# Splits, norms and first gates interleaved between the last expert and the convolution of a two-block transformer kernel

## The reference, cut to what matters

```python
h = h + hier_moe(rmsnorm(h, ffn_norm_g), ...)    # 32 experts, 2 per token
x = rmsnorm(h, final_norm_g)                     # "first norm" of the join
h = rms_norm(x, mix_norm)                        # "second norm" of the join
a, g = jnp.split(h @ w_in + b_in, 2, axis=-1)
u = a * jax.nn.sigmoid(g)
y = silu(layer_norm(causal_conv_31_taps(u) + conv_b)) @ w_out + b_out
x = x + y
x = x + square(relu(rms_norm(x, mlp_norm) @ w1)) @ w2
```

## Time and profile before

| what | value |
| --- | --- |
| median of three runs | 2309.69 us (2308.45 to 2314.13) |
| the profiled execution | 2312.9 us, span 2311.1 us |
| TensorE, busy | 2106.1 us, 91% |
| VectorE, busy | 1263.3 us, 55% |
| ScalarE, busy | 976.7 us, 42% |
| mean granted TensorE clock | 0.959 |
| bytes moved by DMA | 352.96 MB, mean 153 GB/s |

### The profile page before, as it was taken

The page is one execution under the profiler, slowest core; times in us unless marked ns, Lnnn a source line. Parts: engine busy times, 40 slices in busy tenths (PEclk is TensorE's granted clock), DMA queues, the critical chain, the costliest instruction groups (busy, mean ns, idle before and its releaser), DMA issues.

```text
span 2311.1 us, 28597 instructions
## 1 busy us (share of the span) xinstructions
PE 2106.1 (91%) x11035; PEld 1088.9 (47%) x11035; DVE 1263.3 (55%) x1346; ACT 976.7 (42%) x1252; POOL 258.5 (11%) x263
## 2 busy tenths in 40 slices
PE   7988989898499999999936999959899999999999
PEld 5444446644244444444413565634444444444444
DVE  5234247644799898899965253384443343333432
ACT  5212227622388888888754252362322111211210
POOL 0000130000133323233200000041000000000000
PEclk9999999999699999999967999979999999999999
DMA  6110310051399999999974152234211011020001
GB/s 259 37 37 37 91 28 1 19 203 74 120 408 400 402 390 386 385 387 385 371 302 149 50 193 81 76 98 156 73 40 70 36 73 36 36 73 36 36 0 73
DMA packets 74717, 352.96 MB, mean 153 GB/s; under 512 B 16336, under 2 KB 23120, under 8 KB 42064
## 3 DMA queue, kind: packets, MB, share of 16 engines
q1 hardware_dynamic: 56304, 305.21, 34.4%
q0 software_dynamic: 18336, 46.69, 6.2%
HBM read 326.67 MB, written 29.36 MB: 154 GB/s over the span
## 4 chain that ended last, share of the span: by engine, by line
PE 75%; DVE 9%; DMA 7%; issue 4%; ACT 2%; SPq 2%; ACTq 0%; POOL 0%; DVEq 0%; POOLq 0%
PE ps L408 20%; PE ps L410 20%; PE ps L409 20%; DMA stage<-in_w_up 6%; PE pt L408 2%; PE pt L409 2%; PE pt L410 2%; DVE split L538 2%; PE pt L462 1%; DVE cols L1457 1%; SPq L629 1%; PE pt L1870 1%; PE pt L2029 1%; PE pt L2031 1%; PE pt L2030 1%
## 5 line engine op out<-in xcount | busy, mean ns | idle before, releaser
L408 PE MATMUL ps<-xt,split 128*128 128x512 f16 (+1 forms) x992 | 373.6, 377 | 18.0 <-issue 10.4
L408 PE MATMUL ps<-split,xt 128*128 128x512 f16 x928 | 354.5, 382 | 25.5 <-DMA xt<-arena 19.5
L409 PE MATMUL ps<-xt,split 128*128 128x512 f16 (+1 forms) x992 | 373.5, 377 | 0.0
L410 PE MATMUL ps<-xt,split 128*128 128x512 f16 (+1 forms) x992 | 373.3, 376 | 0.0
L409 PE MATMUL ps<-split,xt 128*128 128x512 f16 x928 | 354.5, 382 | 0.0
L410 PE MATMUL ps<-split,xt 128*128 128x512 f16 x928 | 354.3, 382 | 0.0
L538 DVE SCALAR_TENSOR_TENSOR split<-stage,split 128x2048 f16<-128x2048 f32 x128 | 289.6, 2284 | 5.4 <-ACT split L534 5.2
L534 ACT ACTIVATE split<-stage 128x2048 f16<-128x2048 f32 x128 | 243.8, 1909 | 80.5 <-DMA stage<-in_w_up 35.7
L408 PE MATMUL ps<-split,arena 128*128 128x512 f16 x512 | 194.0, 379 | 0.0
L409 PE MATMUL ps<-split,arena 128*128 128x512 f16 x512 | 194.0, 379 | 0.0
L410 PE MATMUL ps<-split,arena 128*128 128x512 f16 x512 | 194.0, 379 | 0.0
(11 more groups left out here) (292 smaller groups left out, 3150.4 us busy)
## 6 DMA issues: line engine op xcount, KB each, us to landing
stage<-in_w_gate SPq DMA_DIRECT2D x64, 1024.0 KB, 11.1
stage<-in_w_up SPq DMA_DIRECT2D x64, 1024.0 KB, 12.1
arena<-in_w_down SPq DMA_DIRECT2D x64, 1024.0 KB, 11.9
stage<-in_w_mlp SPq DMA_DIRECT2D x32, 1024.0 KB, 5.5
arena<-in_conv_taps POOLq DMA_DIRECT2D x32, 576.0 KB, 4.4
stage<-in_w_dense_a SPq DMA_DIRECT2D x16, 1024.0 KB, 7.7
stage<-in_w_dense_b SPq DMA_DIRECT2D x12, 1024.0 KB, 9.9
resid<-in_x SPq DMA_DIRECT2D x16, 512.0 KB, 4.4
```

Of the source, the lines that this page charges most:

```text
L408: nc.tensor.matmul(out_ap, lh, rh, start=start, stop=False)
L409: nc.tensor.matmul(out_ap, lh, rl, start=False, stop=False)
L410: return nc.tensor.matmul(out_ap, ll, rh, start=False, stop=stop)
```

## The change

Four things in the join, and what they need. (1) The units 2 and 3 are loaded ahead of 0 and 1 and split inside the last expert: their high halves before `hTh`, the other two high halves behind it, the four low halves behind the hidden rows' low half. (2) Groups 64 to 67 are cut into pieces of 256 tokens (`piece`), so that products begin when tiles 0 and 1 are there. (3) The lists `JOIN_ACT`, `JOIN_DVE` and `JOIN_PE` write the order out by hand: gates 0 to 3, which read the banks, stand between and behind the norms, and taps 0 to 2 behind gate 2 and gate 3. (4) `UN[k]` is tile k of `H`, so steps k = 0 to 3 need only the stores of tiles 0 to 3 (the store semaphore is now two) and steps k >= 4 no longer wait for `xn`. The squares of the statistics, which were written to `junk` (now in use by the gates), go to slot 3 of `stage`; unit 7 is therefore loaded after the last statistic. SyncE mixes y loads with the stores, and loads the tables before them. A Sqrt on one element stands ahead of the statistics.

```diff
-        UN = [f16_rows(H[:, 4 + k, :]) for k in range(4)] + [f16_rows(xn[:, k % 2, :]) for k in range(4, KT)]
+        UN = [f16_rows(H[:, k, :]) for k in range(KT)]
...
+        JOIN_ACT = seq("one:0 one:1 two:0 two:1 hi:0 hi:1 one:2 two:2 one:3 hi:2 two:3 hi:3 one:4 two:4 one:5 hi:4 "
+                       "two:5 gate:0 one:6 hi:5 two:6 gate:1 one:7 hi:6 two:7 hi:7 gate:2 taps:0 taps:1 gate:3 taps:2")
+        JOIN_DVE = seq("add:0 add:1 one:0 one:1 two:0 two:1 add:2 lo:0 lo:1 one:2 add:3 two:2 one:3 lo:2 two:3 add:4 "
+                       "lo:3 one:4 add:5 two:4 one:5 add:6 lo:4 two:5 gate:0 one:6 add:7 lo:5 two:6 gate:1 one:7 lo:6 "
+                       "two:7 lo:7 gate:2 taps:0 taps:1 gate:3 taps:2")
...
@@ SyncE
-            for m in range(SLOTS):
+            for m in (2, 3, 0, 1):
                 load_b(sp, m)
+            sp.dma_start(tables, a["conv_tables"]).then_inc(s_tab, 16)
+            sp.dma_start(blk, a["c_blk"]).then_inc(s_tab, 16)
...
+            sp.wait_ge(s_moe, 1)
+            for t in range(6):
+                load_y(t)
+            store_x2(0)
+            store_x2(1)
+            load_y(6)
+            store_x2(2)
+            load_y(7)
+            for t in range(3, TT):
+                store_x2(t)
             for m in range(SLOTS, 8):
+                if m == 7:
+                    sp.wait_ge(s_std, 4 * TT + 1)
                 load_b(sp, m)
@@ ScalarE, in the body of an expert
+                else:
+                    for m in (2, 3):
+                        hi_b(act, m)
                 act.wait_ge(s_ht, e + 1)
...
                 nc.scalar.activation(hTh, PS[:, 3, :].rearrange("p (k t) -> p k t", k=4), ACT.Copy)\
                     .then_inc(s_hh, 1)
+                if last and q:
+                    act.wait_ge(s_u, NE)
+                    for m in (0, 1):
+                        hi_b(act, m)
@@ ScalarE, after the experts
-            for m in range(SLOTS):
...
-                hi_b(act, m)
...
+            squares = wstage(3)[:, 0:D]
+            act.wait_ge(s_wo[3], RB + 1)
+            ch.done(nc.scalar.activation(std[:, 0:1], eps, ACT.Sqrt))
...
@@ in input_hi
-                if k >= 4:
-                    act.wait_ge(s_tr, 4 * TT)
-                if k >= 6:
-                    act.wait_ge(s_rb[k - 2], 16 * PH * PH)
+                act.wait_ge(s_x2s[k // 4], 16 * 4)
+                act.wait_ge(s_xn, 3 * TT + k + 1)
@@ VectorE, in the body of an expert
+                if last and q:
+                    for m in (2, 3, 0, 1):
+                        lo_b(dve, m)
@@ TensorE
-            for t in range(TT // 2):
-                transposes(pe, 3, t, from_xn)
+            def piece(g, q):
+                pe.wait_ge(s_free[g % 4], g // 4)
+                pe.wait_ge(s_xl, 3 * TT + 2 * q + 2)
+                c0, tk = (g - 64) // 2 * P, slice(256 * q, 256 * q + 256)
+                for ui in range(2):
+                    u = 2 * (g % 2) + ui
+                    pe.wait_ge(s_wo[u], RB + 1)
+                    for kk in range(UK):
+                        k, c = ui * UK + kk, slice(kk * UC + c0, kk * UC + c0 + P)
+                        i = product(pe, PS[:, g % 4, tk], whi(u)[:, c], wlo(u)[:, c], XH[:, k, tk], XL[:, k, tk],
+                                    k == 0, k == KT - 1)
+                if q:
+                    i.then_inc(s_full[g % 4], 1)
+
+            JOIN_PE = seq("tr:0 tr:1 64:0 65:0 tr:2 66:0 67:0 tr:3 64:1 tr:4 65:1 66:1 tr:5 67:1")
...
             for p, (k, th) in enumerate(GATED):
+                if p < 2:
+                    continue
                 pe.wait_ge(s_xl, 3 * TT + (TT if th else TT // 2))
                 for i in range(2):
                     u = 4 * (k // 4) + 2 * i
                     group_b(pe, 64 + 2 * p + i, (u, u + 1), True, k % 4, th)
-                    for t in {0: (4,), 1: (5, 6), 2: (7,)}.get(2 * p + i, ()):
-                        transposes(pe, 3, t, from_xn)
+                    if p in (2, 3) and i == 0:
+                        transposes(pe, 3, 4 + p, from_xn)
```

More of the change, by code:

```diff
@@ L934, in _ @@
                 phased(k)
[L935 removed]
+            for i in range(2):
+                sp.wait_ge(s_x2s[i], 16 * 4)
             x2_phase = x2_rows.rearrange("(h p r) d -> r h p d", h=2, r=PH)
@@ L1302, in conv_read @@
                         hi_b(act, SPLIT_WITH[k] + q)
-            for n in range(3):
-                taps_hi(n)
-            for p in range(len(GATED)):
+            for what, t in JOIN_ACT:
+                if what == "one":
+                    act.wait_ge(s_cmb, 2 * t + 2)
+                    norm_stats(act, ch, t, squares)
+                elif what == "two":
+                    act.wait_ge(s_x2, t + 1)
+                    norm_stats(act, ch, t, squares)
+                elif what == "hi":
+                    xt_hi(act, 3, t)
+                elif what == "taps":
+                    taps_hi(t)
+                else:
+                    gate(t)
+                    input_hi(t)
+            for p in range(4, len(GATED)):
                 gate(p)
@@ L1555, in body @@
                     .then_inc(s_hl, 1)
-                if not (last and q):
+                if last and q:
+                    for m in (2, 3, 0, 1):
+                        lo_b(dve, m)
+                else:
                     expert_lo(dve, 1, e + 1)
@@ L1644, in conv_sums @@
                         lo_b(dve, SPLIT_WITH[k] + q)
-            for n in range(3):
-                taps_lo(n)
-            for p in range(len(GATED)):
+            for what, t in JOIN_DVE:
+                if what == "add":
+                    add(t)
+                elif what == "one":
+                    first_norm(t)
+                elif what == "two":
+                    second_norm(t)
+                elif what == "lo":
+                    xt_lo(dve, 3, t)
+                elif what == "taps":
+                    taps_lo(t)
+                else:
+                    gated(t)
+            for p in range(4, len(GATED)):
                 gated(p)
@@ L2032, in conv @@
                     nc.tensor.matmul(o, w(wcl, 0), uh, start=False, stop=True).then_inc(s_cf, 1)
+            for what, n in JOIN_PE:
+                if what == "tr":
+                    transposes(pe, 3, n, from_xn)
+                else:
+                    piece(int(what), n)
             for p, (k, th) in enumerate(GATED):
+                if p < 2:
+                    continue
                 pe.wait_ge(s_xl, 3 * TT + (TT if th else TT // 2))
```

86 lines of the change are left out of this document (32 added, 54 removed).

## The result

| kernel | median us | lowest to highest | runs |
|---|---|---|---|
| before, in the same session | 2309.51 | 2308.45 to 2314.13 | 4 |
| changed | 2290.41 | 2288.48 to 2292.87 | 4 |

The ratio is 0.9914, with a 95% interval of 0.9896 to 0.9932: 19.1 us faster, where 24.0 were forecast (2285.7). The range, 2280 to 2297, holds it; the narrower range that the forecast gave for itself, 2281 to 2289, does not. The profiled execution took 2292.87 us (span 2291.0).

What follows compares the result with a forecast made beforehand. It took VectorE's adds and norms, then TensorE, to bound the join; products start 24.0 us earlier, TensorE's stretch stays 78.7, so the profiled 2312.9 becomes 2288.9, or 2285.7 on the runs' scale. Range 2280 to 2297, its own 2281 to 2289.

Steps and rivals of the forecast that it cites:

- What bounds the stretch: Join of last expert and convolution: VectorE's adds and norms of tiles 0 to 3 bind until 1226.66 us, then TensorE.
- Units split in the last expert: Last expert: hidden copy's followers 1.1 us later, four low halves under the store, adds at 1186.5, 1.2 us earlier.
- The 16.2 us from the first add to the first product: VectorE's adds, norms and low halves before TensorE starts sum to 16.2 us; first product at 1202.7, 24.0 us earlier.
- TensorE from the first product on: First product to end of group 75: products, transposes, 5.8 us waits and 5.6 half clock sum to 78.7 us, as before.
- The early start is kept whole: TensorE's stretch stays 78.7 us, so the 24.0 us earlier first product moves the last group from 1305.34 to 1281.4.
- Table loads: ScalarE in the join: four more loads, 5.1 us; two Sqrt loads in VectorE's way, which idles 2.1 us before one:6 and one:7.
- Taps behind gate 3: Taps 2 split until 1269.1, 2.0 us before gate 4 is wanted; TensorE's 7.28 us wait goes, 5.8 of shorter waits come.
- From gate 4 to convolution 0: From gate 4's low half, sixteen DMA issues and a landing take 11.5 us; convolution 0 starts at 1284.7, 24.0 us earlier.
- the one with the late unit 3: Last expert: unit 3 lands only at 1171.0, everything slips 5.5 us more; gain 18.5, 2291.2 us; chance 0.10.
- The long half clock: TensorE stays at half clock for all eight pieces and six transpose sets; gain 8, 2301.6 us; chance 0.07.
- the late VectorE list: VectorE's list binds: six later tiles lose 2 us more each, group 75 ends at 1290.5; gain 15, 2294.9 us; chance 0.10.
- the slower case: TensorE's half clock holds through groups 68 to 71 as well; group 75 12.6 us late, 2322 us; chance 0.04.

Runs made afterwards that it cites:

- second profile: The changed kernel itself run and profiled once more, nothing edited, in a later session: 2291.16 us, ratio 0.9928 against the kernel before.
- experiment 1: Changed kernel with the high and low halves of units 0 to 3 all put back behind the last expert: 2288.85 us, ratio 0.9893.
- experiment 3: Kernel before the change with one edit, taps 2 moved from ahead of gate 0 to behind gate 1: 2302.62 us, ratio 0.9953.
- experiment 4: Changed kernel with groups 64 to 67 whole again, over all 512 tokens, behind the transposes of tile 3: 2295.11 us, ratio 0.9924.
- experiment 5: Changed kernel with gates 0 and 1 behind the last norm's low half, transposes 6 and 7 ahead of group 68: 2302.52 us, ratio 0.9968.
- experiment 7: Changed kernel with high halves behind the hidden copy, VectorE's low halves of units 0 and 1 held until GpSimd's sequencer passed the last store: 2290.21 us.
- experiment 9: Changed kernel with high halves behind the hidden copy, VectorE's low halves of units 0 and 1 held until the last store landed: 2287.76 us.

## Why the prediction was right, and where it was off

The median is 4.7 us above the forecast and outside the forecast's own 2281 to 2289; only the wide range holds it.

1. **What bounds the stretch** (VectorE's adds and norms, then TensorE): right. The main misses are two sizes ahead of the first product, and to which part the gain belongs (5).
2. **Units split in the last expert**, "1.1 us later", adds at 1186.5, "1.2 us before": off. The hidden copy was 2.3 us late, where 1.8 were summed (ScalarE waited for both loads), the low half behind it 1.6 instead of 1.1, the output copy and with it the start of the store 1.65; and GpSimd's index copy took 0.8 longer in one of two profiles, because VectorE's low halves lay beside GpSimd's copy; the prediction put them "under the store" at no cost. First load 2.46 us late (2.43 in the second profile, there with a longer half clock in the down product instead of the longer index copy), first add at 23.97 instead of 22.46: 1.5 us. The price of such an overlap stood in the trace of the kernel before, in its expert loop (last section).
3. **The 16.2 us from the first add to the first product**: measured 19.06. The term left out is the wait for the rows of tile 1, 2.80 us (0.55 in the second profile). In the kernel before these rows landed 8.2 us after the first issue (10.3 here, 8.0 in the second profile), but the adds began 7.1 us after it, behind the low halves, and never saw it. It is the wait that takes the place of the one removed. First product 4.4 us late in all.
4. **TensorE from the first product on**, 78.7: measured 77.85; pauses 5.9 for 5.8, half clock 3.4 for 5.6, the pieces at 0.11 us a matmul for 0.108. The sum hit closer than its parts: the pauses were summed as 2.3, 3.2 and 0.3 and came as 2.49, 1.09, 0.34 and 1.97. They make up for one another because VectorE's list sets the times: in experiment 1 the 2.49 us pause was followed by full clock, and the next pause was not 1.09 but 2.76 us, with half clock behind it (row below); that window was 78.05 us. Dividing the groups cost nothing, as said. One remark in that part was wrong: pieces of 256 columns do occur in the kernel before, in its first stage.

```profile
1228.11 1.97 PE L463 MATMUL pt<-misc,xn 128*128 128x128 f32 x8 [2.76 <-DVE xn L1618]
```

5. **"The early start is kept whole"**, the early first product as the main term: the sum is right, the attribution is not. Experiments 3, 4 and 5 take it apart. Taps 2 alone give 9.7 us; the pieces added without the early gates 0.1 to 1.6 more, as an estimate; gates and taps without the pieces 17.0 of 20.4. Taking the early bank reads out of the whole costs 10.7 to 12.9 us, taking out the pieces 3.5 to 5.7 (against the two profiles of the changed kernel). Each pays only where the next wait is gone as well: pieces fill four banks and stop there, and gates between norms are what lets TensorE go on.
6. **Table loads**: right, VectorE's waits were 1.95 and 1.96 where 2.1 were said, and a load costs 1.27.
7. **Taps behind gate 3**: right. The high half of taps 2 ends at 1273.3, its low half at 1274.7, and gate 4's product waits 1.66 us for TensorE, not for it.
8. **From gate 4 to convolution 0**, 11.5 us: measured 11.46. **Gain after convolution 0**: none beyond the spread of the profiles, as said.

Of the rivals, the one with the late unit 3 has the nearest time (2291.2), but its mechanism came only in small part: ScalarE waited 0.58 us for unit 3 and the hidden copy slipped 0.5 us more than summed, where the rival has everything behind it 5.5 us later. That its time fits is luck; the loss has other terms (2 and 3). The long half clock, the late VectorE list and the slower case did not occur. Of the prediction's signs of being wrong three showed: the add that waits for its rows, ScalarE held on unit 3, and `lo:7` past its mark (1263.06, that is 1261.3 on the prediction's scale, against 1261), the last because the first product was late: from that product on it came after 54.3 us where 55.1 were summed.

## What to carry to other kernels

When a wait is removed, ask when each of the inputs behind it lands, not only the first: tile 1's rows had been hidden by the work that was moved away. A piece of a change is priced by undoing it in the changed kernel as well as by making it alone, since parts that open one bank, one engine and one load after another pay only together. And VectorE's free time beside a GpSimd instruction on the critical path is not free: keep it silent until the store has landed, or leave the work where it was. Before work is moved beside another engine's instruction, look in the trace at hand for places where the two already overlap.

## What the runs showed of the hardware

GpSimd's index copy of 128 x 1 takes 0.18 us while VectorE is silent, and 0.98 and 1.44 when it starts inside a low half (two inputs in SBUF), ending with it to within 0.05 us. The indirect issue takes 0.97 alone and 2.54 and 2.97 when it starts inside one, ending 0.86 and 0.9 after the end of that instruction, although in experiment 7 the next low half then runs; VectorE's own 2.29 us do not grow. The kernel before shows both already, with VectorE's and GpSimd's rows of its experts:

```profile
1158.70 2.29 DVE L538 SCALAR_TENSOR_TENSOR arena<-arena 128x2048 f16<-128x2048 f32 x1 [3.09 <-ACT arena L534]
1159.61 1.43 POOL L1014 COPY cols<-cols 128x1 int32<-128x1 int32 x1 [10.46 <-ACT arena L1225]
...
674.97 2.29 DVE L538 SCALAR_TENSOR_TENSOR arena<-arena 128x2048 f16<-128x2048 f32 x1
675.98 2.18 POOL L1017 DMA_INDIRECT y_rows<-arena,cols  x1 [0.88 <-POOL cols L1014]
```

Of its 63 index copies the 39 that take 0.34 us or more all begin inside a low half and end with one; of its 32 indirect issues of expert rows the 28 that begin inside a low half take 2.16 to 2.18 us and end 0.9 us after it, the other four 0.97 to 1.02. The 19 copies that begin inside L1554, which has one input in PSUM, all take 0.18 (the first at 633.02). It looks like a wait for the running instruction and not like a sharing of bandwidth; only one copy, at 639.70, was held through two low halves in a row (3.69 us). The Trainium skill ("SBUF — State Buffer", Who interferes with whom) says that a VectorE instruction with two SBUF inputs holds up a GpSimd instruction that reads SBUF, and the copy agrees; it infers, for `tensor_tensor`, that this does not hold up the writing of descriptors, and the indirect issue, which reads its row numbers from SBUF, differs.

In the changed kernel the clock fell to half (0.51) 0.7 us after a pause of 2.49 us (1225.34), and a pause of 1.97 us (1248.41) was followed by full clock. In experiment 1 the clock stayed full behind a 2.49 us pause (1222.57) and was half behind the next, of 2.76 (1228.11); in experiment 9 it fell behind the 1.97 us pause too. So the length of the last pause alone does not tell.
